# Attention stage of a two-block layer on one core: exponentials scaled by GpSimd, rotary scores on four row quarters

## The reference, cut to what matters

```python
# A heads (chunks of 64 queries against their own and up to 8 chunks before them)
sc = jnp.einsum('bihd,bjhd->bhij', q_blk, kb).astype(jnp.float32) * scale + bias[None]
sc = jnp.where(valid[None, None, None, :], sc, NEG_INF)
p = jax.nn.softmax(sc, axis=-1).astype(vb.dtype)
o = jnp.einsum('bhij,bjhd->bihd', p, vb)
...
# B heads
q_full = jnp.concatenate([q_nope, q_pe], axis=-1)
k_full = jnp.concatenate([k_nope, jnp.broadcast_to(k_pe, (b, s, B_HEADS, B_ROPE))], axis=-1)
sc = jnp.einsum('bqhd,bkhd->bhqk', q_blk, k).astype(jnp.float32) * scale
sc = jnp.where(mask[None, None], sc, NEG_INF)
p = jax.nn.softmax(sc, axis=-1).astype(v.dtype)
o = jnp.einsum('bhqk,bkhd->bqhd', p, v)
...
x = x + jnp.concatenate([out_a, out_b], axis=-1) @ w_out[l]
```

## Time and profile before

| | |
|---|---|
| median of 3 executions | 1700.57 us (1699.32 to 1702.35) |
| the profiled execution | 1701.04 us, span 1699.2 us |
| PE, busy share | 98% |
| PEld | 80% |
| DVE | 56% |
| ACT | 25% |
| POOL | 58% |
| mean granted TensorE clock | 0.991 of full |
| chain that ended last | 93% PE |

### The profile page before, as it was taken

One profiled execution on the slowest core, in us unless ns is written; L12 is line 12 of the kernel. 1 busy time (PEld: TensorE's weight loads), 2 busy tenths in 40 slices (PEclk: granted clock), 3 DMA queues, 4 the chain that ended last, 5 costly groups with the idle time before them and its releaser, 6 DMA issues.

```text
span 1699.2 us, 26804 instructions
## 1 busy us (share of the span) xinstructions
PE 1657.6 (98%) x10118; PEld 1355.5 (80%) x10118; DVE 946.7 (56%) x1389; ACT 433.2 (25%) x721; POOL 981.4 (58%) x596
## 2 busy tenths in 40 slices
PE   8999999999999999999999999998989999999998
PEld 6888888888767778888888867887868788888887
DVE  5666551226656346666562159987766766665103
ACT  4000000015866321111100031234353333233001
POOL 3666666766572377666677744611205576666774
PEclk9999999999999999999999989999999899999999
DMA  6444443333241134444443322210002232233332
GB/s 215 142 147 148 146 144 118 102 100 121 87 120 33 50 106 143 142 147 148 148 150 111 100 87 70 92 64 3 3 2 87 75 96 92 97 99 99 101 110 88
DMA packets 52112, 175.43 MB, mean 103 GB/s; under 512 B 6272, under 2 KB 8704, under 8 KB 51904
## 3 DMA queue, kind: packets, MB, share of 16 engines
q1 hardware_dynamic: 43056, 144.64, 26.3%
q10 hardware_dynamic: 8976, 29.63, 5.5%
HBM read 169.46 MB, written 2.10 MB: 101 GB/s over the span
## 4 chain that ended last, share of the span: by engine, by line
PE 93%; ACT 2%; DVE 2%; issue 1%; POOL 1%; DMA 0%; ACTq 0%; SPq 0%; DVEq 0%; POOLq 0%
PE banks L730 25%; PE banks L732 25%; PE banks L731 25%; PE banks L1199 4%; PE banks L1055 1%; PE banks L1028 1%; PE banks L762 1%; PE banks L1039 1%; PE banks L763 1%; PE banks L768 1%; PE banks L850 1%; PE banks L1025 1%; PE banks L1174 1%; PE banks L803 1%; PE banks L805 0%
## 5 line engine op out<-in xcount | busy, mean ns | idle before, releaser
L602 POOL TENSOR_TENSOR w_lo<-w_raw,w_hi 128x1024 fp32r<-128x1024 f32 x256 | 634.2, 2477 | 21.4
L600 POOL TENSOR_SCALAR w_hi<-w_raw 128x1024 fp32r<-128x1024 f32 x256 | 288.4, 1126 | 555.5 <-DMA w_raw<-in_slabs 477.0
L730 PE MATMUL banks<-h_hi,w_hi 128*128 128x512 f32 x1376 | 540.6, 393 | 0.6 <-POOL w_lo L602 0.6
L732 PE MATMUL banks<-h_hi,w_lo 128*128 128x512 f32 x1376 | 535.7, 389 | 0.0
L731 PE MATMUL banks<-h_lo,w_hi 128*128 128x512 f32 x1376 | 535.6, 389 | 0.0
L730 PEld LDWEIGHTS banks<-h_hi,w_hi 128*128 128x128 f32 x1376 | 258.4, 188 | 60.2 <-issue 5.8
L731 PEld LDWEIGHTS banks<-h_lo,w_hi 128*128 128x128 f32 x1376 | 258.4, 188 | 54.4 <-issue 1.7
L732 PEld LDWEIGHTS banks<-h_hi,w_lo 128*128 128x128 f32 x1376 | 258.3, 188 | 54.1
L730 PE MATMUL banks<-act_hi,w_hi 128*128 128x512 f32 (+1 forms) x550 | 209.7, 381 | 0.0
L731 PE MATMUL banks<-act_lo,w_hi 128*128 128x512 f32 (+1 forms) x550 | 209.3, 381 | 0.0
L732 PE MATMUL banks<-act_hi,w_lo 128*128 128x512 f32 (+1 forms) x550 | 209.3, 381 | 0.0
(11 more groups left out here) (389 smaller groups left out, 1840.8 us busy)
## 6 DMA issues: line engine op xcount, KB each, us to landing
w_raw<-in_slabs SPq DMA_DIRECT2D x260, 512.0 KB, 3.5
adaw<-in_ada ACTq DMA_DIRECT2D x48, 512.0 KB, 3.6
relb<-in_relb ACTq DMA_DIRECT2D x8, 256.0 KB, 2.9
out_y<-xT SPq DMA_DIRECT2D x16, 128.0 KB, 1.8
w_raw<-in_slabs SPq DMA_DIRECT2D x4, 256.0 KB, 5.2
...
```

The costliest lines, as they stand in the source:

```text
L600: nc.gpsimd.tensor_scalar(w_hi[:, r, :], w_raw[:, r, :], 1.0, 1.0, ALU.mult, ALU.mult).then_inc(S("w_hi"), 1)
L602: nc.gpsimd.tensor_tensor(w_lo[:, r, :], w_raw[:, r, :], w_hi[:, r, :], ALU.subtract).then_inc(S("w_split"), 1)
L730: mm(out, hi, rhs_hi, start=start, stop=False, skip_group_check=True)
L732: return mm(out, lo, rhs_hi, start=False, stop=stop, skip_group_check=True)
```

## The change

The exponentials themselves are now multiplied by the reciprocals, by GpSimd, before they are transposed (`probs_scaled`). `recips_widened`, `recips_spread`, `keep_recips` and `out_scaled` are gone; `out_hi` and `out_lo` read the value bank directly, which alternates between 6 and 7 by pair. The B heads' steps go by two pairs at a time: steps 16, 17 are query block 0 of pairs 4 and 5, steps 18, 19 block 1 of both, and so on. PE issues the scores of two such steps in one go: the plain part as 64-row products, like the A heads', and then the rotary part of all four heads as 32-row products on rows 0, 32, 64 and 96, added into the same banks (`rotary_scores`). `rows_moved` goes; SP copies the rotary key rows to the three other row quarters. The B heads use six buffers of `prob` by turns instead of four (two lie in `relb`). GpSimd's rotary instructions are taken apart, one behind each of steps 4 to 6, 8 to 10 and 12 to 14.

```diff
         def pair_step(t):
-            p, qb = divmod(t, NT)
+            if t < 4 * NT:
+                p, qb = divmod(t, NT)
+            else:
+                two, r = divmod(t - 4 * NT, 2 * NT)
+                p, qb = 4 + 2 * two + r % 2, r // 2
             return p, qb, P * (qb + 1)
+        def last_step(p):
+            return NT * p + NT - 1 if p < 4 else 4 * NT + 2 * NT * (p // 2 - 1) - 2 + p % 2
...
-            def rows_moved():
-                for p in range(4):
-                    sp.wait_ge(S("scores"), 2 * NT * (p + 1))
...
+            def key_rows_copied():
+                sp.wait_ge(S("roped"), 3)
+                for a in range(32, P, 32):
+                    sp.dma_start(kr[a:a + 32, 0, :], kr[0:32, 0, :]).then_inc(S("key_rows"), 16)
...
-            def recips_widened(t):
...
-                nc.gpsimd.tensor_scalar(out, rec_of(t).unsqueeze(2).to_broadcast([P, 2, CH]), 1.0, None, ALU.mult)                    .then_inc(S("recips"), 1)
+            def probs_scaled(t):
                 pool.wait_ge(S("row_recip"), t + 1)
+                for e in range(2):
+                    nc.gpsimd.tensor_scalar(prob_of(t, e), prob_of(t, e), rec_of(t)[:, e:e + 1], None, ALU.mult)\
+                        .then_inc(S("prob_scaled"), 1)
...
-            rope_applied(0)
-            for t in range(8 * NT):
-                if t == NT:
-                    rope_applied(1)
-                    rope_applied(2)
-                    pool.wait_ge(S("roped"), 9)
-                recips_widened(t)
+            for t in range(2, 8 * NT):
+                probs_scaled(t)
+                if NT <= t < 4 * NT and t % NT < 3:
+                    rope_applied(t // NT - 1, t % NT)
...
-            def recips_spread(p):
-                pe.wait_ge(S("recips"), NT * p + NT)
-                if p:
-                    pe.wait_ge(S("o_kept"), 2 * p - 1)
-                for qb in range(NT):
-                    b = slice(P * qb, P * qb + P)
-                    last = nc.tensor.transpose(bank[7][:, b], rec_wide[p % 2][:, b], ident)
-                last.then_inc(S("rows_spread"), 1)
...
+                q, k = (qa, ka) if p < 4 else (qn, kn)
                 for e in range(2):
-                    mm(out[e][:, 0:L], head_rows(qn, p - 4, e)[:, qs], head_rows(kn, p - 4, e)[:, 0:L], start=True, stop=True)\
-                        .then_inc(S("scores"), 1)
+                    e64 = slice(CH * e, CH * e + CH)
+                    last = mm(score_bank(t, e)[:, 0:L], q[e64, p % 4, qs], k[e64, p % 4, 0:L], start=True, stop=p < 4,
+                              skip_group_check=True)
+                    if p < 4:
+                        last.then_inc(S("scores"), 1)
+            def rotary_scores(t):
+                p, qb, L = pair_step(t)
+                if t == 4 * NT:
+                    pe.wait_ge(S("key_rows"), 48)
+                pe.wait_ge(S("roped"), 6 if p < 6 else 9)
+                for i in range(4):
+                    r = slice(32 * i, 32 * i + 32)
+                    mm(score_bank(t + i // 2, i % 2)[:, 0:L], qr[r, (p - 4) // 2, P * qb:P * qb + P], kr[r, 0, 0:L],
+                       start=False, stop=True, skip_group_check=True).then_inc(S("scores"), 1)
...
             def turn(t):
-                    pe.wait_ge(S("probs"), 2 * t + e + 1)
+                    pe.wait_ge(S("prob_scaled"), 2 * t + e + 1)
...
             def values(t):
-                if qb == 0 and p >= 1:
-                    pe.wait_ge(S("o_made"), 2 * p - 1)
+                if qb == 0 and p >= 2:
+                    pe.wait_ge(S("o_made"), p - 1)
...
             for i in range(8 * NT + 3):
-                if 3 <= i + 1 < 8 * NT:
+                if 3 <= i + 1 < 4 * NT:
                     scores(i + 1)
+                elif 4 * NT <= i + 1 < 8 * NT and (i + 1) % 2 == 0:
+                    scores(i + 1)
+                    scores(i + 2)
+                    rotary_scores(i + 1)
-                if i >= 6 and i % NT == 2:
-                    recips_spread((i - 6) // NT)
...
-                if 8 * NT - 1 <= i < 8 * NT + 2:
-                    out1_begun(i - (8 * NT - 1))
+                if i >= 8 * NT - 1 and i != 8 * NT + 1:
+                    out1_begun((8 * NT - 1, 8 * NT, 8 * NT + 2).index(i))
...
-            def keep_recips(p):
...
             def out_hi(p):
-                act.wait_ge(S("o_made"), 2 * p + 1)
-                f(h_hi[:, p, :], o_scaled, ACT.Copy).then_inc(S("o_kept"), 1)
+                act.wait_ge(S("values"), last_step(p) + 1)
+                f(h_hi[:, p, :], bank[6 + p % 2], ACT.Copy).then_inc(S("o_kept"), 1)
...
+                for p in range(8):
+                    if i == last_step(p) + 4:
+                        out_hi(p)
...
-            def out_scaled(p):
...
             def out_lo(p):
-                dve.wait_ge(S("o_kept"), 2 * p + 2)
-                v.tensor_tensor(h_lo[:, p, :], o_scaled, h_hi[:, p, :], ALU.subtract).then_inc(S("o_made"), 1)
+                dve.wait_ge(S("o_kept"), p + 1)
+                v.tensor_tensor(h_lo[:, p, :], bank[6 + p % 2], h_hi[:, p, :], ALU.subtract).then_inc(S("o_made"), 1)
...
-            for i in range(3, 8 * NT + 5):
+            for i in range(3, 8 * NT + 4):
                 if i < 8 * NT:
                     score_max(i)
                 if 5 <= i < 8 * NT + 3:
                     keep_turned(i - 3)
-                if i >= 7 and i % NT == 3:
-                    out_scaled((i - 7) // NT)
-                if i >= 8 and i % NT == 0:
-                    out_lo((i - 8) // NT)
-                for t in range(3) if i == 3 else range(i - 1, min(i, 8 * NT)):
-                    row_recip(t)
+                if 4 <= i < 8 * NT + 1:
+                    row_recip(i - 1)
+                for p in range(8):
+                    if i == last_step(p) + 4:
+                        out_lo(p)
```

89 lines of the change are left out of this document (32 added, 57 removed).

## The result

| | before | after |
|---|---|---|
| median | 1700.43 us (1699.32 to 1702.35, 4 executions) | 1710.35 us (1709.85 to 1711.35, 4 executions) |
| the profiled execution | 1701.04 us, span 1699.2 us | 1710.56 us, span 1708.8 us |
| the stage (see below) | 102.97 us | 112.62 us |

The changed kernel is slower: the ratio of the times is 1.0059, 95% interval 1.0045 to 1.0073, 9.9 us by the medians. The forecast was 1697.6 us in a range of 1694.0 to 1706.0.

A forecast was written before the change was run, and what follows sets the result against it. PE, busy 98% of the span, was taken as the bound; -3.6 - 2.9 + 0.9 - 0.7 + 2.8 = -3.5 us from the median 1700.57, plus 0.5 for unpriced items, gave 1697.6 us, range 1694.0 to 1706.0.

The forecast's parts named there:

- Part 5: GpSimd's new scalings: 0.25 to 0.62 us each by length, 7.3 us per pair with rotary steps, under PE's 8.5.
- (a): GpSimd's scaling is dear, PE waits at the 512 steps' transposes: 1705.9 us at two-input price, 1715 at L621's; chance 0.26.
- two ends of the bound: Low and high price of one GpSimd scaling at 512 columns: 0.62 us by L610, 1.75 by L621.
- turning point: GpSimd's price that uses up the gain: from about 1.0 us per 512 scaling; slower by 0.2% from about 1.25.
- two-input case: GpSimd's scaling at a two-input price, 1.28 us at 512 columns: 8 us of waits in all, 1705.9 us.
- (b): No new waits of PE in the stage, the PE terms alone: -6.3 us, 1694.3 us; chance 0.14.
- (c): Second-half 32-row products don't run four at once: 1701.9 us two at a time, 1710.4 one at a time; chance 0.08.
- Part 1: The widened reciprocals' transposes go, four per pair: 3.6 us less on PE.
- Part 2: Scores of the last four pairs in bursts of two steps, 16.0 us instead of 18.9: 2.9 us less.
- Part 6: New PE waits for DVE's copies and minima and for GpSimd: 1.2 us first half, 1.6 second, 2.8 in all.
- Part 3: Second-half transposes now always follow another row mode, 0.66 us instead of 0.60: 0.9 us more on PE.
- Part 4: PE's waits for DVE's product in bank 6 (0.28 us) and for h_lo (0.41) go: 0.7 us less.

The follow-up runs named there:

- e1: The changed kernel with GpSimd's scalings written with two factors (reciprocal, then 1.0) instead of one; 1699.25 us, ratio 0.9991 to the kernel before.
- e8: The changed kernel with GpSimd's scaling written as a two-input product, the reciprocal column broadcast; 1698.46 us, ratio 0.9988 to the kernel before.
- e11: e1 with the one-factor scaling at the 512-column steps alone; 1702.65 us, ratio 1.0007 to the kernel before.

## Why the prediction was wrong, point by point

**Part 5 failed, and alone decided the sign.** It took L610's price (0.62 us at 512 columns) over L621's (1.75) because the new form "reads plain rows as L610 does", and blamed L621's spread source. The choice went by the shape of the operands, when the number of factors was what the two rows differed in: it measured 1.56. Had the end been taken by the instruction's arguments, the sum would have had the 17 us more that rival (a) gives for L621's price; the runs showed 11.35 (e1 against the changed kernel). The two ends of the bound were right, and so was the sentence that the only one-factor row is L621; the weight given to it was not.

**The rivals.** (a) was what happened, at nearly L621's price: 1715 there, 1710.35 measured. Its mechanism holds: GpSimd's work over a pair is longer than PE's, though by 12.2 against 9.3 us and not by 13.0 against 8.5. Its place holds for 4.5 of the 8.2 us of waits; the other 3.7 stand at 384 steps, which it didn't name. Its turning point doesn't hold: "from about 1.0 us" measured as no cost at 1.04 (e8), and its two-input case of 1705.9 came out at 1698.5. The step at fault set GpSimd's work over a pair against PE's 8.5 us, where a pair with its waits for DVE takes 9.3, and it left out that the two scalings of one long step can be late while GpSimd still has idle time (e11). (b) fell: the waits were there. (c) fell: four 32-row products of 512 columns took 1.07 us. The Trainium skill ("TensorE: Matmul & The Clock Gate", Part 3) has a factor of 3.07 for such a block, from which the prediction estimated 1.25 us. Worked again with a stream time of 0.85 it is 4 x 0.85 / 3.07 = 1.11 us, or 1.31 with the 0.2 for the mode, both estimates; by the first the trace nearly agrees (4 x 0.85 / 1.07 = 3.2), by the second it doesn't.

**Part 1 was right:** the transposes of the reciprocals took 3.76 us from start to start before (all 32 of them), of which some 0.15 passes to the transposes behind them, as predicted: 3.6.

**Part 2 was right in mechanism and nearly in size:** bursts of 1.08, 1.71, 2.35 and 2.99 us against 1.04, 1.68, 2.32 and 2.96; 16.4 instead of 16.0 for the eight, so 2.5 us less instead of 2.9. In the 16.4 is a second 384 burst of 2.49 us: the weights of its second step wait for DVE's minimum. That is the place where Part 6 had a wait of 0.6; it costs 0.14, and no row of PE's waits shows it.

**Part 3 was right and Part 4 nearly:** the transposes behind a burst read 0.66 a row of four records, as in the earlier trace rows, and the waits of the earlier trace rows are gone. But the second of these was a wait of a weight load: PE's products there start 0.38 us apart where they otherwise start 0.23 apart, so it was worth 0.15 and not 0.41, and the two together some 0.5 instead of 0.7. PE's timeline of before at that place:

```profile
582.99 0.39 PE L732 MATMUL banks<-h_hi,w_lo 128*128 128x512 f32 x1
583.37 0.50 PE L730 MATMUL banks<-h_hi,w_hi 128*128 128x512 f32 x1
```

**Part 6 had the right chain and the wrong size of it, and who waits.** In e1, where GpSimd is out of the way, the three waits of the first half are 0.59, 0.57 and 0.53 us, 1.7 and some 0.5 beside them, where 1.2 was predicted with 0.3 of it for GpSimd; it is the second head's transposes that wait, half a step before the values that I had named. The second half measured 1.16 us in five waits, about 2.0 with what is beside them, against 1.6. The 0.17 beside each wait had no row; the forecast had 0.5 us for everything unpriced. With them e1's stage should change by -3.6 - 2.5 + 0.9 - 0.5 + 2.85 + 8 x 0.17 = -1.5 us; it changed by -1.7.

**In place of the sum.** -1.7 us as in e1, and 11.35 for GpSimd's price: 8.0 in the three pairs in which GpSimd has no rest (28.76 to 36.76 us between the same instructions of PE), 1.05 ahead of them and 2.3 behind; +9.65 us. That the clock could fall below full was named as what would make the forecast wrong altogether. It did fall, but while PE was held up by GpSimd, and by GpSimd's rows that cost at most 0.16 us.

**The tests named beforehand worked.** POOL's row at 128x512 (1562 instead of 620 ns) and the sum of PE's waits for POOL (8.2 instead of under 1 us) each told (a) from the first profile.
